# Gamma row written as 16 rows, modulation pieces spread anew, 1/rms per token block, the output projection's second half by chunk, and a moved DMA-queue wait, in a two-layer mLSTM / attention / GLA block kernel

## The chip, the cores and the metric

One NeuronCore of one Trainium2 chip runs the whole program in one launch. The metric is the device time of an execution in microseconds. Three executions of the kernel before took 2641.11, 2654.57 and 2652.0 us; their median is 2652.0 us.

## What is computed

Two layers over 256 tokens of width 2048, batch 1, all fp32. A conditioning vector gives six modulation vectors per layer; each layer is a mixer and a convolutional feed-forward, both between modulated RMS norms:

```python
cond = jax.nn.silu(c)
for layer in range(2):
    mod = (cond @ ada_w[layer] + ada_b[layer])[:, None, :]
    sh_m, sc_m, g_m, sh_f, sc_f, g_f = jnp.split(mod, 6, axis=-1)
    h = rms_norm(x, norm_w[layer, 0]) * (1.0 + sc_m) + sh_m
    y = even_mixer(h, ...) if layer == 0 else odd_mixer(h, ...)
    x = x + g_m * rms_norm(y, norm_w[layer, 1])
    h = rms_norm(x, norm_w[layer, 2]) * (1.0 + sc_f) + sh_f
    y = conv_ffn(h, ...)
    x = x + g_f * rms_norm(y, norm_w[layer, 3])
```

`even_mixer` is an mLSTM (4 heads) beside a forgetting attention (8 heads); `odd_mixer` is gated linear attention (GLA, 4 heads) with a low-rank decay gate. `conv_ffn` is a 2048 to 2x5632 projection, a causal three-tap depthwise convolution, `a * gelu(g)`, and a projection back.

## The kernel before

**Units.** All projection weights are cut into 394 units of 128x2048 fp32 (1 MB). A unit goes through a fixed chain. The SP queue loads it into one of four `raw` slots. ACT rounds it to fp32r (`hi`, L458). DVE writes the rest (`lo = raw - hi`, L851). PE multiplies `hi` by the high and low part of the activations and `lo` by the high part. There are two slots of `hi` and `lo`, so the `hi` of unit n+1 waits until PE has finished unit n-1 (`s_unit`). In every loop body step j, DVE first makes the `lo` of the *next* unit, then does whatever else belongs to step j, and last copies PE's result out of PSUM. A unit of kind "columns" (or `ff_up`) has 48 matmuls of 256 columns (L1539 to L1541); a unit of kind "tokens" (`values`, `mixed`, `ff_down`) has 24 of 512 columns (L1564 to L1566).

**Phases.** The table in `plan()` lists the phases in order; every engine walks the same table. Per layer: gates, the mixer's input projections with the mixer's own work beside them (`side`), `mixed` (the mixer's output projection, 16 units), and then three groups of `ff_up` and `ff_down` (32+16, 32+16 and 24+12 units). `ff_down` makes four chunks of 512 output columns, four units each (three in the last group). `mixed` makes its four chunks two at a time: its units alternate between chunk 0 and 1, then between 2 and 3, so that chunks complete at units 6, 7, 14 and 15 (`token_unit`).

**Modulation.** `ada_w` is cut into 384 pieces of 128x1024 (0.5 MB; 32 pieces make one of 12 sections). The first 64 are summed at the start of the program from eight slots. The other 320 are loaded into two slots (`piece`) and summed by DVE (L862, 1.2 us each) inside the phases; the fifth argument of a phase says how many in each step. In SP's queue the load of piece a+2 waits until piece a is summed (`s_mac`), and it stands behind that step's unit load. While the GLA phases run, the piece buffers hold GLA data: no pieces are summed from `PAUSE` on until `mixed` of layer 1, where SP waits for `gla_stored` before it loads two pieces anew.

**Post-norm and pre-norm.** In `mixed` and in the last `ff_down` group (the phases with `ph.sums`), ACT squares and sums each completed chunk (`square_y`, L530) and DVE multiplies it by `gamma` (`by_gamma`, L948). `gamma` (modulation gate times norm weight) lies as 128x16, channel k*128+p at partition p, and has to become a row of 2048 on every partition. ACT's queue writes it to DRAM (`gamma_row_dmas`, L539: 2048 values of 4 bytes each) and reads it back to all partitions (L542, 1 MB). The read waits on ACT for the write (`s_row_out`). ACT runs this in its own program order, between two `hi` operations: the write at step 5, the wait and the read at step 6.

After the last unit DVE reduces the squares, adds the scaled `y` to `x` in five pieces (L965), ACT squares `x` (L483, five pieces), DVE sums them over both token blocks (`x_root`, L897), ACT takes the root (L471), DVE the reciprocal and two diagonal matrices (L902). PE multiplies `x` by them: this transposes and scales at once (`x_transposes`, L1379), 24 blocks before the next phase's first unit. ACT and DVE apply the modulation (`scaled`, L494 and L913) and split the result (`high`, `low`, L504 and L920), and the first unit starts when the first pair is ready.

```python
if j == 5:
    sc.wait_ge(s_gamma, m + 1)
    with nc.allow_non_contiguous_dma("2048 values, once for each norm"):
        sc.dma_start(row_dram.rearrange("a (k p) -> p (a k)", p=P), gamma[:, :]).then_inc(s_row_out, 16)
if j == 6:
    sc.wait_ge(s_row_out, 16 * (m + 1))
```

## Time and profile before

| | |
|---|---|
| executions | 2641.11, 2654.57, 2652.0 us |
| profiled execution | 2654.36 us, span 2652.6 us |
| PE busy | 2402.4 us (91%) |
| PE weight loads busy | 2216.4 us (84%) |
| DVE busy | 1963.7 us (74%) |
| ACT busy | 1019.7 us (38%) |
| TensorE clock granted, mean | 0.965 of full |
| bytes moved | 627 MB, mean 236 GB/s |

PE is the busiest engine, and the share hides where it stops. The time is best read as a chain of phases, each of which either runs at PE's pace or at that of something that PE waits for. The profiled execution took 2.4 us more than the median.

### The profile page before, as it was taken

The numbers are of one execution on the slowest core, as the hardware profiler recorded it, in microseconds if no ns is written. First come the engines' busy times: TensorE is split into PE (matmuls) and PEld (weight loads), VectorE is DVE, ScalarE is ACT, GpSimd is POOL, SyncE is SP. The second block draws the span as 40 slices with busy tenths as digits, with TensorE's granted clock in tenths as the row PEclk, the third lists the DMA queues.
The fourth block names the chain that finished last, engine by engine and source line by source line (L and its number), as shares of the span: only waits on it lengthen the run. The fifth ranks groups of instructions, "written<-read, shape, count | busy, mean of one in ns | idle before, by whom it ended". The sixth has DMA issues, their size and how long they took to land.

```text
span 2652.6 us, 40622 instructions
## 1 busy us (share of the span) xinstructions
PE 2402.4 (91%) x16118; PEld 2216.4 (84%) x16118; DVE 1963.7 (74%) x2340; ACT 1019.7 (38%) x1001; POOL 426.2 (16%) x198
## 2 busy tenths in 40 slices
PE   0499999879999999999959999977899999999996
PEld 0488878669997999889949989966899899989994
DVE  7876886679997899789867776656899556655654
ACT  1223434444343343333435544433443334333442
POOL 0000000003430244014200000000234013411320
PEclk9799998989999999999979999989899999999997
DMA  9888774666778877887866644456577555455553
GB/s 400 337 311 293 278 273 179 197 226 236 271 284 301 288 280 268 327 291 274 280 213 244 234 157 144 143 165 249 182 275 271 191 190 186 177 190 191 185 181 94
DMA packets 122601, 627.16 MB, mean 236 GB/s; under 512 B 20960, under 2 KB 21088, under 8 KB 71280
## 3 DMA queue, kind: packets, MB, share of 16 engines
q1 hardware_dynamic: 113648, 621.22, 65.2%
q10 hardware_dynamic: 8832, 4.23, 0.6%
q8 instruction: 88, 1.44, 0.2%
q14 instruction: 33, 0.27, 0.0%
HBM read 623.27 MB, written 2.13 MB: 236 GB/s over the span
## 4 chain that ended last, share of the span: by engine, by line
PE 74%; DMA 12%; DVE 11%; ACT 2%; issue 1%; SPq 0%; DVEq 0%; ACTq 0%
PE bank L1539 16%; PE bank L1540 16%; PE bank L1541 16%; DMA piece<-ada_pieces 8%; PE bank L1564 7%; PE bank L1565 7%; PE bank L1566 7%; DVE lo L851 3%; DVE piece L862 3%; DVE region L862 1%; PE bank L1379 1%; DMA region<-ada_pieces 1%; ACT hi L458 1%; PE bank L1456 1%; DMA gamma_scratch<-gamma 1%
## 5 line engine op out<-in xcount | busy, mean ns | idle before, releaser
L458 ACT ACTIVATE hi<-raw 128x2048 fp32r<-128x2048 f32 x394 | 754.3, 1915 | 1323.6 <-PE bank L1541 794.5
L1539 PE MATMUL bank<-act,hi 128*128 128x256 f32 x3872 | 1105.2, 285 | 11.6 <-DVE lo L851 10.5
L1540 PE MATMUL bank<-act,hi 128*128 128x256 f32 x3872 | 1098.3, 284 | 0.0
L1541 PE MATMUL bank<-act,lo 128*128 128x256 f32 x3872 | 1098.2, 284 | 0.0
L851 DVE TENSOR_TENSOR lo<-raw,hi 128x2048 fp32r<-128x2048 f32 x394 | 901.7, 2289 | 237.4 <-ACT hi L458 236.8
L1539 PEld LDWEIGHTS bank<-act,hi 128*128 128x128 f32 x3872 | 746.1, 193 | 17.7 <-DVE lo L851 13.1
L1540 PEld LDWEIGHTS bank<-act,hi 128*128 128x128 f32 x3872 | 746.2, 193 | 0.3
L1541 PEld LDWEIGHTS bank<-act,lo 128*128 128x128 f32 x3872 | 745.8, 193 | 0.0
L862 DVE SCALAR_TENSOR_TENSOR piece<-piece,cond 128x1024 f32<-128x1024 f32 x320 | 452.2, 1416 | 130.5 <-DMA piece<-ada_pieces 129.9
L832 POOL TENSOR_TENSOR region<-region 128x256 f32<-128x256 f32 x88 | 204.7, 2327 | 1063.2 <-ACT region L732 1063.2
L1564 PE MATMUL bank<-hi,mid 128*128 128x512 f32 x704 | 276.9, 393 | 35.5 <-DVE lo L851 35.5
L1565 PE MATMUL bank<-lo,mid 128*128 128x512 f32 x704 | 275.4, 391 | 0.0
L1566 PE MATMUL bank<-hi,mid 128*128 128x512 f32 x704 | 275.1, 391 | 0.0
L835 POOL TENSOR_TENSOR mid<-region,mid 128x256 f32 (+1 forms) x88 | 207.6, 2359 | 276.1 <-ACT mid L736 276.1
L1564 PE MATMUL bank<-hi,act 128*128 128x512 f32 x512 | 209.0, 408 | 38.7 <-DVE lo L851 37.1
L1565 PE MATMUL bank<-lo,act 128*128 128x512 f32 x512 | 204.9, 400 | 0.0
L1566 PE MATMUL bank<-hi,act 128*128 128x512 f32 x512 | 204.2, 399 | 0.0
L1564 PEld LDWEIGHTS bank<-hi,mid 128*128 128x128 f32 x704 | 133.1, 189 | 67.2 <-DVE lo L851 39.9
L1379 PE MATMUL bank<-region,x 128*128 128x128 f32 x256 | 41.9, 335 | 145.4 <-DVE region L902 111.8
L1326 DVE TENSOR_SCALAR region<-bank,vec 128x256 f32<-128x256 f32 x176 | 95.2, 541 | 99.5 <-PE bank L1541 95.7
L1379 PEld LDWEIGHTS bank<-region,x 128*128 128x128 f32 x256 | 40.3, 249 | 146.9 <-issue 65.9
L1566 PEld LDWEIGHTS bank<-hi,mid 128*128 128x128 f32 x704 | 133.0, 189 | 28.0
(155 smaller groups left out, 1562.4 us busy)
## 6 DMA issues: line engine op xcount, KB each, us to landing
raw<-w_units SPq DMA_DIRECT2D x394, 1024.0 KB, 4.8
piece<-ada_pieces SPq DMA_DIRECT2D x320, 512.0 KB, 4.9
region<-ada_pieces SPq DMA_DIRECT2D x64, 512.0 KB, 8.7
region<-gamma_scratch ACTq DMA_DIRECT2D x4, 1024.0 KB, 7.8
x<-x_in SPq DMA_DIRECT2D x1, 2048.0 KB, 15.5
x_out<-x SPq DMA_DIRECT2D x3, 512.0 KB, 2.8
cond<-c_row SPq DMA_DIRECT2D x1, 1024.0 KB, 4.4
vec<-vectors SPq DMA_DIRECT2D x1, 534.5 KB, 11.0
```

What stands on the lines that cost most here:

```text
L458: sc.activation(hi[:, slot, :], raw[:, raw_slot, :], ACT.Copy).then_inc(s_hi, 1)
L832: gp.tensor_tensor(ff_m[:, slot, :], conv_a[:, slot, :], gelu_g[:, slot, :], ALU.mult).then_inc(s_mul, 1)
L835: gp.tensor_tensor(flat(mid[:, at_, T:2 * T]), ff_m[:, slot, :], flat(mid[:, at_, 0:T].bitcast(F32)), ALU.subtract).then_inc(s_mid, 1)
L851: ve.tensor_tensor(lo[:, slot, :], raw[:, raw_slot, :], hi[:, slot, :].bitcast(F32), ALU.subtract).then_inc(s_lo, 1)
L862: return ve.scalar_tensor_tensor(out=src, in0=src, scalar=1.0, in1=cond[:, half * PIECE:(half + 1) * PIECE], op0=ALU.mult, op1=ALU.mult, a ...
L1379: i_ = pe.matmul(bank[4 + p % 4][:, at:at + P], x[:, tb, kt * P:(kt + 1) * P], diag[:, tb, :], start=True, stop=True)
L1539: pe.matmul(dst, w_hi, act[:, kt, 0:T], start=at == 0, stop=False)
L1540: pe.matmul(dst, w_hi, act[:, kt, T:2 * T], start=False, stop=False)
L1541: i_ = pe.matmul(dst, w_lo, act[:, kt, 0:T], start=False, stop=at == DK - 1)
L1564: pe.matmul(dst, x_hi, w_hi, start=opens and q == 0, stop=False)
L1565: pe.matmul(dst, x_hi, w_lo, start=False, stop=False)
L1566: i_ = pe.matmul(dst, x_lo, w_hi, start=False, stop=closes and q == 3)
```

## The change

Seven edits, all in the order of the work; no arithmetic of the reference changes.

1. **Gamma by 16 rows.** PE transposes `gamma` into PSUM after step 1 of the phase, DVE copies the 16x128 block to SBUF (step 2 in `mixed`, step 3 in `ff_down`), ACT's queue writes it as 16 rows of 128 values at step 3, and waits and reads it back at step 5. `gate_weight` of `mixed` moves from step 4 to step 0.
2. **`by_gamma`** of chunks 0 to 2 moves from behind the copies to fixed steps (`late_gamma`).
3. **`mixed`** becomes one body of 16 steps: 8 as before, then chunk 2 in four units and chunk 3 in four.
4. **Pieces.** Another number per step in eight phases; `PAUSE` moves from 336 to 344.
5. **1/rms per token block**: `x_root` becomes `x_sum` and `x_diag`, one of each per block, between the updates of `x`; PE transposes block 0 of the first eight channel tiles before block 1 (`x_first_transposes`).
6. DVE's `lo` of the second unit of a phase with a pre-norm moves behind the pre-norm.
7. **SP's wait** for `gla_stored` moves from before `mixed` of layer 1 to its step 3, behind that step's unit load.

```diff
-        if self.kind == "mixed":
+        if self.kind == "mixed" and j < 8:
             return j % 2, tail(self)[0][j // 2], j < 2, j >= 6
         tile, g = divmod(j, self.k_units)
...
-    no, half = (0,) * 4, (2, 1) * 4
+    no, down = (0,) * 4, (1, 2, 2, 1) * 4
...
-              Phase("values", 0, 1, 8, (1,) * 8, dest=M_HEADS * M_DV),
+              Phase("values", 0, 1, 8, (2, 1) * 4, dest=M_HEADS * M_DV),
...
-              Phase("mixed", 0, 2, 8, (0, 1, 0, 0, 1, 2, 2, 2)),
-              Phase("ff_up", 0, 8, 4, (1,) * 4, 0), Phase("ff_down", 0, 2, 8, half, 0),
-              Phase("ff_up", 0, 8, 4, (1,) * 4, 1), Phase("ff_down", 0, 2, 8, half, 1),
-              Phase("ff_up", 0, 6, 4, (1,) * 4, 2), Phase("ff_down", 0, 1, 12, (1, 2, 1) * 4, 2),
+              Phase("mixed", 0, 1, 16, (0, 0, 0, 0, 1, 1, 1, 1, 1, 2, 2, 1, 1, 1, 0, 0)),
+              Phase("ff_up", 0, 8, 4, (1,) * 4, 0), Phase("ff_down", 0, 1, 16, down, 0),
+              Phase("ff_up", 0, 8, 4, (1,) * 4, 1), Phase("ff_down", 0, 1, 16, down, 1),
+              Phase("ff_up", 0, 6, 4, (1,) * 4, 2),
+              Phase("ff_down", 0, 1, 12, (1, 2, 2, 1, 2, 2, 1, 2, 2, 1, 0, 0), 2),
               Phase("gates", 1, 1, 1, (0,)),
-              Phase("columns", 1, 4, 4, (2, 1, 2, 1), dest=GQ, side="decay"),
+              Phase("columns", 1, 4, 4, (2,) * 4, dest=GQ, side="decay"),
...
-              Phase("mixed", 1, 2, 8, (0, 0, 0, 0, 1, 2, 2, 3)),
+              Phase("mixed", 1, 1, 16, (0, 0, 0, 0, 0, 1, 1, 1, 1, 1, 1, 1, 1, 0, 0, 0)),
...
+                        if ph.a0 == PAUSE and ph.kind == "mixed" and j == 3:
+
+                            sp.wait_ge(s["gla_stored"], G_HEADS)
+                            for more in range(ADA_SLOTS):
+                                load_piece(PAUSE + more, more)
...
                     sc.activation(yt[:, tb, at:at + size], x[:, tb, at:at + size], ACT.Square,
                                   accum_out=stat[:, col:col + 1]).then_inc(s_xsq, 1)
+                    if k == 1:
+                        token_root(S_RHO, 1)
+                token_root(S_RHO + 1, 1)
...
+                if j == 3:
+                    sc.wait_ge(s_rows, m + 1)
+                    sc.dma_start(row_dram.rearrange("a (k p) -> (a k) p", p=P), gamma_rows).then_inc(s_row_out, 16)
                 if j == 5:
-                    sc.wait_ge(s_gamma, m + 1)
-                    with nc.allow_non_contiguous_dma("2048 values, once for each norm"):
-                        sc.dma_start(row_dram.rearrange("a (k p) -> p (a k)", p=P), gamma[:, :]).then_inc(s_row_out, 16)
-                if j == 6:
+                    if ph.kind == "mixed":
+                        sc.wait_ge(*((s["mlstm_stored"], 2 + M_HEADS) if ph.layer == 0 else (s["gla_stored"], G_HEADS)))
                     sc.wait_ge(s_row_out, 16 * (m + 1))
...
-                for tb, at, size in X_PIECES:
+                for k, (tb, at, size) in enumerate(X_PIECES):
+                    if k == 3 and not last:
+                        x_sum(m + 1, 0)
                     x_at = x[:, tb, at:at + size]
                     ve.scalar_tensor_tensor(out=x_at, in0=yt[:, tb, at:at + size], scalar=r[:, tb:tb + 1], in1=x_at,
                                             op0=ALU.mult, op1=ALU.add).then_inc(s_x, 1)
+                if not last:
+                    x_diag(m + 1, 0)
+                    x_sum(m + 1, 1)
+                    x_diag(m + 1, 1)
...
                 if ph.norms:
+                    pre_norm(ph)
                     if ph is not PHASES[0]:
-                        x_root(2 * ph.layer + int(ph.kind == "ff_up"))
                         split_next(ph, 0, 0)
-                    pre_norm(ph)
...
+                late_gamma = (8, 9, 13) if ph.kind == "mixed" else (7, 8, 10)
...
+                        if ph.sums:
+                            if j == (2 if ph.kind == "mixed" else 3):
+                                gamma_to_rows(ph)
+                            if j in late_gamma:
+                                by_gamma(ph, late_gamma.index(j))
...
+            def x_first_transposes(q):
+                for tb in range(TB):
+                    pe.wait_ge(s_diag, TB * q + tb + 1)
+                    for kt in range(DK // 2):
+                        i_ = x_block(kt // 2, kt, tb)
+                        if tb == TB - 1 and kt % 2 == 1:
+                            i_.then_inc(s_tp, 1)
...
+                        if ph.sums and j == 1:
+                            pe.wait_ge(s_gamma, 2 * ph.layer + int(ph.kind == "ff_down") + 1)
+                            pe.transpose(bank[4][0:DK, 0:P], gamma[:, :], ident[:, :]).then_inc(s_gt, 1)
```

ACT in the last `ff_down` of layer 0, before. `hi<-raw` is the split of a unit's weights; `region,stat<-y` the squares of a chunk:

```order
L458 ACTIVATE hi<-raw 128x2048 x2
L530 ACTIVATE region,stat<-y 128x512 x2
L458 ACTIVATE hi<-raw 128x2048 x2
L539 DMA gamma_scratch<-gamma 128x16x1
L458 ACTIVATE hi<-raw 128x2048
L542 DMA region<-gamma_scratch 128x2048
L530 ACTIVATE region,stat<-y 128x512 x2
L458 ACTIVATE hi<-raw 128x2048 x3
```

And with the change:

```order
L461 ACTIVATE hi<-raw 128x2048 x2
L544 DMA gamma_scratch<-region 16x128
L536 ACTIVATE region,stat<-y 128x512 x2
L461 ACTIVATE hi<-raw 128x2048 x2
L549 DMA region<-gamma_scratch 128x2048
L461 ACTIVATE hi<-raw 128x2048
L536 ACTIVATE region,stat<-y 128x512 x2
```

The write stands two splits earlier, and two splits lie between write and read instead of one.

DVE from the last step of `mixed` of layer 0 into the pre-norm of `ff_up`, before (`piece,part` is a modulation piece, `y<-bank` the copy of a chunk):

```order
L851 TENSOR_TENSOR lo<-raw,hi 128x2048
L862 SCALAR_TENSOR_TENSOR piece,part<-piece,cond 128x1024
L1306 COPY y<-bank 128x512 x2
L948 TENSOR_TENSOR y<-y,region 128x2x512
L862 SCALAR_TENSOR_TENSOR piece,part<-piece,cond 128x1024
L948 TENSOR_TENSOR y<-y,region 128x512
L958 TENSOR_REDUCE stat<-stat 128x2
...
L965 SCALAR_TENSOR_TENSOR x<-y,stat,x 128x1024 x3
L965 SCALAR_TENSOR_TENSOR x<-y,stat,x 128x512 x2
L897 TENSOR_REDUCE stat<-stat 128x2
L884 RECIPROCAL stat<-stat 128x2
L902 TENSOR_SCALAR region<-ident,stat 128x128 x2
```

With the change:

```order
L857 TENSOR_TENSOR lo<-raw,hi 128x2048 x2
L1335 COPY y<-bank 128x512 x2
L959 TENSOR_TENSOR y<-y,region 128x512
L970 TENSOR_REDUCE stat<-stat 128x2
...
L979 SCALAR_TENSOR_TENSOR x<-y,stat,x 128x1024 x3
L902 TENSOR_REDUCE stat<-stat 128x1
L979 SCALAR_TENSOR_TENSOR x<-y,stat,x 128x512 x2
L890 RECIPROCAL stat<-stat 128x1
L908 TENSOR_SCALAR region<-ident,stat 128x128
L902 TENSOR_REDUCE stat<-stat 128x1
```

Two pieces and one full `by_gamma` left the stretch between the last unit and the updates, and the first diagonal matrix is ready before the squares of block 1 are summed.

SP around `mixed` of layer 1, before (what stands in brackets is what the issue waits for):

```order
L402 DMA raw<-w_units 128x2048 [waits lo_ready] x33
L406 DMA piece<-ada_pieces 128x1024 [waits gla_stored]
L406 DMA piece<-ada_pieces 128x1024
L402 DMA raw<-w_units 128x2048 [waits lo_ready] x5
```

With the change:

```order
L406 DMA raw<-w_units 128x2048 [waits lo_ready] x37
L410 DMA piece<-ada_pieces 128x1024 [waits gla_stored]
L410 DMA piece<-ada_pieces 128x1024
L406 DMA raw<-w_units 128x2048 [waits lo_ready] x2
```

Four more unit loads stand ahead of the wait.

## Rows read from the trace of the kernel before

**Rows 1.** The page: GB/s in 40 slices; the chain that ended last, by engine.

```profile
GB/s 400 337 311 293 278 273 179 197 226 236 271 284 301 288 280 268 327 291 274 280 213 244 234 157 144 143 165 249 182 275 271 191 190 186 177 190 191 185 181 94
...
PE 74%; DMA 12%; DVE 11%; ACT 2%; issue 1%; SPq 0%; DVEq 0%; ACTq 0%
```

**Rows 2.** Who waited for whom: us in total, times, longest.

```profile
PE bank L1379 <- DVE region L902: 111.8, 4, 65.9
...
PE bank L1564 <- DVE lo L851: 72.6, 17, 15.0
```

**Rows 3.** Stretches: length, busy time PE PEld DVE ACT POOL, clock, DMA, GB/s.

```profile
117.33:221.53 104.20, 95.76 (x771) 94.12 (x769) 76.95 (x92) 34.17 (x21) 0.00 (x0) 0.98 0.84 299
221.53:269.49 47.96, 45.77 (x197) 37.12 (x195) 33.05 (x37) 15.50 (x9) 0.00 (x0) 0.96 0.79 283
466.95:571.13 104.18, 92.21 (x384) 73.97 (x384) 68.03 (x66) 39.01 (x34) 0.00 (x0) 0.95 0.68 227
...
781.27:874.50 93.23, 89.01 (x387) 71.36 (x385) 69.69 (x75) 31.38 (x18) 3.69 (x2) 1.00 0.87 310
...
1289.33:1371.43 82.10, 67.08 (x290) 54.87 (x288) 53.39 (x56) 29.12 (x28) 3.51 (x2) 0.92 0.82 266
...
1400.64:1497.76 97.12, 97.12 (x786) 95.01 (x785) 72.84 (x84) 51.81 (x48) 0.00 (x0) 1.00 0.76 283
1728.74:1848.90 120.16, 96.41 (x394) 77.62 (x392) 65.70 (x62) 39.48 (x35) 0.00 (x0) 0.90 0.60 201
...
2558.09:2640.27 82.18, 67.84 (x290) 55.43 (x288) 32.73 (x23) 27.07 (x27) 3.15 (x2) 0.90 0.37 115
2332.79:2419.86 87.07, 87.07 (x386) 72.08 (x385) 42.04 (x25) 31.50 (x18) 3.15 (x2) 1.00 0.54 193
...
2148.48:2332.79 184.31, 184.31 (x1537) 184.31 (x1536) 119.98 (x127) 71.86 (x62) 71.32 (x30) 1.00 0.51 183
```

**Rows 4.** The chain that ended last, last ff_down of layer 0: start, us, what.

```profile
1316.84 14.45 DMA gamma_scratch<-gamma
1331.31 7.80 DMA region<-gamma_scratch
```

**Rows 5.** Timeline, mixed of layer 1: start, us, what, [idle before, releaser].

```profile
1761.83 1.91 ACT L458 ACTIVATE hi<-raw 128x2048 fp32r<-128x2048 f32 x1 [12.72 <-DMA raw<-w_units]
...
1766.12 0.80 PE L1564 MATMUL bank<-hi,act 128*128 128x512 f32 x1 [8.14 <-DVE lo L851]
...
1787.71 0.80 PE L1564 MATMUL bank<-hi,act 128*128 128x512 f32 x1 [8.93 <-DVE lo L851]
```

**Rows 6.** DMA issues: KB each, median us from issue to landing.

```profile
piece<-ada_pieces SPq DMA_DIRECT2D x320, 512.0 KB, 4.9
...
x_out<-x SPq DMA_DIRECT2D x3, 512.0 KB, 2.8
...
gamma_scratch<-gamma ACTq DMA_DIRECT2D x4, 8.0 KB, 14.2
```

**Rows 7.** Timeline from the last unit of mixed, layer 0.

```profile
573.92 1.28 DVE L1306 COPY y<-bank 128x512 f32<-128x512 f32 x2
...
579.37 5.00 DVE L965 SCALAR_TENSOR_TENSOR x<-y,stat,x 128x1024 f32<-128x1024 f32 x5
...
582.85 0.19 ACT L483 ACTIVATION_READ_ACCUMULATOR y<-x 128x1 f32 x1
...
586.75 7.85 PE L1379 MATMUL bank<-region,x 128*128 128x128 f32 x48 [15.46 <-DVE region L902]
```

**Rows 8.** Timeline, the transposes at the other two norms.

```profile
1383.96 8.57 PE L1379 MATMUL bank<-region,x 128*128 128x128 f32 x48 [12.37 <-DVE region L902]
...
1867.04 7.71 PE L1379 MATMUL bank<-region,x 128*128 128x128 f32 x48 [17.98 <-DVE region L902]
```

**Rows 9.** Timeline of DVE behind that pre-norm of layer 0.

```profile
599.00 2.48 DVE L920 TENSOR_TENSOR act<-y,act 128x512 fp32r<-128x512 f32 x4
...
604.92 2.29 DVE L851 TENSOR_TENSOR lo<-raw,hi 128x2048 fp32r<-128x2048 f32 x1 [0.43 <-ACT hi L458]
```

More of the change, by code:

```diff
@@ L435, in _ @@
                     sp.dma_start(g_w2, w2_dram).then_inc(s["loaded_a_w2"], 16)
-                if ph.a0 == PAUSE and ph.kind == "mixed":
-                    sp.wait_ge(s["gla_stored"], G_HEADS)
-                    for k in range(ADA_SLOTS):
-                        load_piece(PAUSE + k, k)
                 straight = ph.per_body > 0 and ph.a_end in (PAUSE, SECTIONS * PIECES)
@@ L939, in gate_weight, with gamma_to_rows @@
                                  ALU.mult).then_inc(s_gamma, 1)
+            def gamma_to_rows(ph):
+                m = 2 * ph.layer + int(ph.kind == "ff_down")
+                ve.wait_ge(s_gt, m + 1)
+                ve.tensor_copy(gamma_rows, bank[4][0:DK, 0:P]).then_inc(s_rows, 1)
             def by_gamma(ph, chunk, first=0, last=TB):
@@ L952, in post_norm @@
             def post_norm(ph, between):
+                last = ph is PHASES[-1]
                 m = 2 * ph.layer + int(ph.kind == "ff_down")
@@ L1233, in _ @@
                 if sec > 0:
-                    x_root(0)
+                    ve.wait_ge(s_in["ident"], 16)
+                    x_sum(0, 0)
+                    x_diag(0, 0)
+                    x_sum(0, 1)
+                    x_diag(0, 1)
                     ve.wait_ge(s_in["vec"], 16)
@@ L1309, in body @@
                             i_.then_inc(s_evac, 1)
-                            if ph.sums and ph.tiles * i + tile > 0:
-                                by_gamma(ph, ph.tiles * i + tile - 1)
                         elif ph.kind == "gates":
@@ L1369, in _, with x_block @@
         def _(pe):
+            def x_block(p, kt, tb):
+                at = (kt % 2) * T + tb * P
+                return pe.matmul(bank[4 + p % 4][:, at:at + P], x[:, tb, kt * P:(kt + 1) * P], diag[:, tb, :],
+                                 start=True, stop=True)
+            def x_first_transposes(q):
[5 more added lines that the diff above has]
+                            i_.then_inc(s_tp, 1)
             def x_transposes(q, p):
-                if p >= 4 and p % 2 == 0:
+                if p % 2 == 0:
                     pe.wait_ge(s_na, 4 * q + (p - 4) // 2 + 1)
-                if p >= 4 and p % 2 == 1:
+                else:
                     pe.wait_ge(s_nv, 4 * q + (p - 4) // 2 + 1)
@@ L1377, in x_transposes @@
                     for tb in range(TB):
-                        at = (kt % 2) * T + tb * P
-                        i_ = pe.matmul(bank[4 + p % 4][:, at:at + P], x[:, tb, kt * P:(kt + 1) * P], diag[:, tb, :],
-                                       start=True, stop=True)
+                        i_ = x_block(p, kt, tb)
                 i_.then_inc(s_tp, 1)
@@ L1514, in _ @@
                     q = 2 * ph.layer + int(ph.kind == "ff_up")
-                    pe.wait_ge(s_diag, q + 1)
-                    for p in range(6):
+                    x_first_transposes(q)
+                    for p in (4, 5):
                         x_transposes(q, p)
```

36 lines of the change are left out of this document (18 added, 18 removed).

## The prediction

> **What bounds the kernel now.** I read the page first. The chain that ended last is PE for 74% and DMA for 12% [rows 1]: PE sets the pace, and the question is where it stops. The view of waits names two stops. PE's first matmul of a token unit waits for DVE's `lo`, 72.6 us in all, and the norm transposes wait for the diagonal matrices, 111.8 us, of which 65.9 us are one harmless early wait [rows 2]. To price phases I took the pace of phases in which nothing is late: 16 token units in 87.07 us, 5.44 each, and 32 column units in 184.31 us, 5.76 each [rows 3]. What a phase takes beyond that is loss:
>
> - `mixed` of layer 0: 104.18 - 87.07 = 17.1
> - last `ff_down` of layer 0 (12 units, 65.3 at pace): 82.10 - 65.3 = 16.8
> - `mixed` of layer 1: 120.16 - 87.07 = 33.1
> - last `ff_down` of layer 1: 82.18 - 65.3 = 16.9 [rows 3].
>
> Three norm transitions follow, each with PE idle for 12.4 to 18.0 us before the transposes and 8 us of transposes [rows 7, 8].
>
> **Gamma.** The chain through the last `ff_down` of layer 0 is a write of 14.45 us and then the read-back of 7.80 [rows 4]. ACT waits in between and cannot split the next weights, so PE starves; clock is lost too (0.92 and 0.90 granted in these stretches against 1.00 [rows 3]). The new write moves the same 8 KB in 16 rows. The trace has no such DMA: the write of 4-byte values took 14.2 us, a store of 512 KB in long rows 2.8 us [rows 6]. I take 3 us, by the latter, since it differs from the old in its rows and not in its bytes; it may also be shorter or as long as before. From step 3 to the wait at step 5 are two units, 10.9 us, and the readers of the row come 2 or 3 units after that, 10.9 us or more against 7.8. So both waits end before anybody is there: the 16.8 and 16.9 go. New on this path are a transpose and a copy of 16 rows, under 0.5 us, beside other work, and in `ff_down` ACT waits at step 3 for the copy that stands behind DVE's `lo`, with its next split about 1 us late and as much slack: 0.2 each. **-33.3.**
>
> The Trainium skill, in DMA: Bandwidth & Descriptors, section Anatomy of one DMA, puts the fixed cost of a DMA at about 2.0 us, most of it the receipt of the write. By it the new write would take 2.0 us; no row here shows one, and the sum would be the same.
>
> **`mixed` of layer 0.** Of the 17.1 some 3 are the gating work of its first steps and stay. The rest, near 13.7, is the same 14 us write and the pieces that land late beside it (one, two, two and two in steps 4 to 7). It goes, but `gate_weight`, the copy and the write's issue now stand in the tight steps (0.7), and steps 9 and 10 sum two pieces each beside a `by_gamma` (1.5). **-11.5.**
>
> **`mixed` of layer 1.** Two causes. SP waits for `gla_stored` before all loads of the phase: ACT waited 12.72 us for `raw`, PE 8.14 [rows 5], with the cold clock after it 9.8 in all. Behind the new place of the wait four more units are already loading, and the last GLA head is stored in step 3 or 4, one unit before the first withheld load matters: the 9.8 go. Then the gamma write and up to three pieces a step: 8.93 once [rows 5] and 6.7 again eight units on, with their slow restarts 21.4. These go as well, since each step has one piece. About 2 remain, and 1.3 are new (the last gating part collides with a split). **-29.9.**
>
> **Transitions.** In layer 0 the last unit of `mixed` ends at 571.13 [rows 3]. DVE copies its chunk only at 573.92, since a piece is late, and begins the updates 5.45 us after that [rows 7], with `by_gamma` of chunk 2 (1.2) and a piece (1.2) in between. With neither left the copy starts at once (0.2), and the updates about 3.7 us later, as the squares of the last chunk are now waited for: 3.9 after the unit. Updates to transposes took 7.4 us (579.37 to 586.75). Now block 0 is squared 3.7 us after the updates begin (582.85 + 0.19), its sum lies between the third and the fourth update, which end with the fifth at 5.2, and reciprocal, diagonal and start add 0.7: 5.9. ACT's root delays the squares of block 1 by 0.7 us; its diagonal is due at 8.0, while the eight transposes of block 0 keep PE until 8.5 at least (7.85 / 24 = 0.33 us each on average, more at first, when PE comes from idling and has the lower clock). So PE resumes 9.8 us after the unit, where it took 15.6; 9.4 where it took 12.5 (last `ff_down`, no section to close), and 9.8 where it took 18.1 (layer 1) [rows 8]. The same 24 blocks follow, 7.8 us. Together 5.8 + 3.1 + 8.3, **-17.2**.
>
> Against that stands the `lo` that moved behind the pre-norm. It was made while DVE waited for transposes, at no cost. DVE ends the pre-norm at 601.4, and the second unit started near 602.7 (2.2 us before the `lo` of the third, at 604.92) [rows 9]. Now 2.2 us of `lo` come first, 603.6, so each such phase starts its second unit 1.0 later, three times: **+3.0.** It is bounded by 0 and 2.2 each.
>
> **The end.** One `by_gamma` less after the last copy, largely replaced by the wait for the squares: **-0.5.** At the start DVE must wait between the two diagonals for ACT's squares of block 1, about 2.9 us, but the piece loads queued ahead cover it and DVE then sums faster than they land: **+0.5**, at most 2.9.
>
> **Pieces.** What left `mixed` has gone elsewhere. With two slots, a slot's cycle is a load (4.9 us, median [rows 6], up to 7 beside a unit load) and a sum of 1.2.
>
> - `values` of layer 0, 8 to 12 pieces, 1.5 a unit. `ff_down` has this density: 93.23 - 87.07 = 6.2 lost in 16 units [rows 3]. Half of it, **+3**, bounds 0 and 6.
> - The two `ff_down` with (1, 2, 2, 1) in place of (2, 1, 2, 1): the same number, but two double steps in a row leave a slot one unit of 5.44 us for its cycle. **+1 each**, bounds -2 and +5.
> - Last `ff_down` of layer 0, 16 pieces in 10 units instead of 12. At the 3.9 us a piece (93.23 / 24) they need 62 us where PE needs 54, less what two slots already hold: **+5**, bounds 1 and 10.
> - `decay` columns of layer 1, 24 to 32 pieces, two a unit. The first column phase of layer 0 has just this and takes 104.20 us for 16 units; this one takes 97.12 [rows 3]. I take about 105: **+8**, and 1 for the later start of GLA, bounds 2 and 14.
>
> The slices of the page show 400 GB/s at the start [rows 1], so two pieces and a unit, 2.1 MB, would fit into 5.3 us; what limits is the cycle of the slots. The Trainium skill speaks otherwise, in DMA: Bandwidth & Descriptors, section Where 436 GB/s comes from: HBM gives a core some 358 GB/s. The trace disagrees, with its 400; by the page this phase would be bound at 5.86 us a unit and cost 1.6 instead of 8.
>
> **Sum.** -33.3 - 11.5 - 29.9 - 17.2 - 0.5 = -92.4, and 3 + 0.5 + 3 + 2 + 5 + 9 = +22.5: **-69.9**. Against the profiled execution's 2654.4 that is 2584.5; the median lies 2.4 below it, so I say **2582**.
>
> **Rivals.** *The pieces cost twice as much.* DVE, SP and the queue are in order, and a late piece delays the next `lo`: for it speaks that losses in `ff_down` come from waits for pieces, against it that PE has a unit of slack here and there. The 19 us of pieces become 38: 2601. Chance 0.17.
>
> *The write stays slow* (12 us or more, since it is a write to DRAM and not its rows that cost). ACT then waits some 4 us at step 5 in four phases, 3.5 each on PE: 2596. The store of 2.8 us speaks against it. Chance 0.08.
>
> *The stalls return cheaper than I think*, with PE's clock up all through `mixed` and denser pieces hidden: the piece terms vanish, 2563. Chance 0.13.
>
> *Slower than before:* the slot cycle becomes the bound. Some 108 of the pieces lie in phases with 1.5 or more a unit (12 + 24 + 24 + 16 + 32); two slots make each microsecond of cycle worth half a microsecond a piece, 54 us. It would take 83 us on top, 1.5 us on every cycle, to pass 2652 by 0.5%: 2665 or more. Nothing shows such a cycle, 8 us on average. Chance 0.01.
>
> *The change doesn't do what it says:* the row still comes late, since ACT stands at step 3 behind PE's transpose and DVE's copy for a unit or more. Gamma's term would halve: 2600, within the range; 0.03.
>
> **Numbers.** My own case has 0.58, with its bounds 2566 to 2598. The range of 0.8 takes in the cheap rival in part and most of the dear ones: 2562 to 2604. A measurement of this kernel tells about 0.5% (13 us) from no change: faster 0.97, same 0.02, slower 0.01.
>
> **What would show it.** Right: the write `gamma_scratch` under 4 us; no idle of PE above 3 us inside any `mixed` or last `ff_down`; the two `mixed` at 93 and 90 us, the last `ff_down` of layer 0 and 1 at 70 and 66; PE's idle before the transposes 9.5 us three times; first units of these phases near 9 us; `decay` at 105. Wrong: a new wait of ACT at step 3 or 5, PE idle behind pieces over 40 us in sum, or transposes that wait for the second diagonal.

## The result and the profile after

Four executions of the changed kernel took 2576.94 to 2580.99 us, median 2579.84, beside 2649.7 for the kernel before on the same chip. The ratio is 0.9738, 95% interval 0.971 to 0.9766: faster, by about 70 us. The prediction was 2582 (2562 to 2604). The profiled execution took 2580.99 us, span 2579.2, against 2654.36 and 2652.6 before: 73.4 us less.

The page of the changed kernel, GB/s in 40 slices and the chain by engine, against [rows 1]:

```profile
GB/s 397 339 316 305 286 286 197 214 209 266 271 272 323 294 275 271 307 300 277 287 266 226 297 147 147 132 178 279 187 274 272 196 182 185 186 181 195 180 184 141
...
PE 73%; DMA 11%; DVE 11%; ACT 2%; issue 1%; DVEq 0%; SPq 0%; ACTq 0%
```

The shares of the chain have hardly moved, and the page alone would not show where 73 us went. The stretches do. The view of windows, columns as in [rows 3]; in this order: `values` and `mixed` of layer 0, `ff_down` groups 0 and 1 of layer 0, the last `ff_down` of layer 0, the decay columns, `mixed` of layer 1, the last `ff_down` of layer 1:

```profile
221.07:270.76 49.69, 46.24 (x194) 37.12 (x195) 36.53 (x42) 14.72 (x8) 0.00 (x0) 0.97 0.84 308
465.88:556.42 90.54, 88.16 (x385) 71.75 (x385) 68.95 (x64) 38.76 (x34) 0.00 (x0) 1.00 0.69 256
762.08:853.67 91.59, 88.11 (x386) 71.58 (x384) 69.50 (x75) 32.55 (x19) 3.69 (x2) 1.00 0.87 316
1038.08:1130.54 92.46, 88.33 (x387) 71.59 (x385) 69.79 (x75) 33.13 (x19) 3.37 (x2) 1.00 0.86 312
1269.10:1344.47 75.37, 69.20 (x291) 55.12 (x289) 55.48 (x60) 28.88 (x28) 3.69 (x2) 0.95 0.82 299
1369.91:1475.28 105.37, 99.83 (x784) 96.73 (x785) 78.75 (x97) 51.00 (x48) 0.00 (x0) 0.98 0.89 302
1711.33:1800.63 89.30, 89.30 (x395) 73.41 (x393) 62.69 (x54) 39.28 (x35) 0.00 (x0) 1.00 0.68 247
2502.22:2567.70 65.48, 65.48 (x291) 53.89 (x289) 34.23 (x25) 27.09 (x27) 3.15 (x2) 1.00 0.39 144
```

Read each length against its row in [rows 3]. `mixed` of layer 0 fell from 104.18 to 90.54 and that of layer 1 from 120.16 to 89.30; in the latter PE is now busy for the whole stretch, at the full granted clock, where it had 0.90. The last `ff_down` of layer 1 fell from 82.18 to 65.48, its pace. That of layer 0 fell by 6.7 only and keeps a clock of 0.95: something still stops PE there. The decay columns grew from 97.12 to 105.37.

DMA issues, KB each and median us to landing, against [rows 6]:

```profile
region<-gamma_scratch ACTq DMA_DIRECT2D x4, 1024.0 KB, 7.1
...
gamma_scratch<-region ACTq DMA_DIRECT2D x4, 8.0 KB, 3.3
```

The write of the same 8 KB takes 3.3 us in the median where it took 14.2; the four of this execution took 1.9 to 5.1 us.

The norm transition of layer 0, timeline, against [rows 7] (the last unit of `mixed` ends at 556.42):

```profile
556.62 1.29 DVE L1335 COPY y<-bank 128x512 f32<-128x512 f32 x2 [1.14 <-PE bank L1604]
...
560.08 3.68 DVE L979 SCALAR_TENSOR_TENSOR x<-y,stat,x 128x1024 f32<-128x1024 f32 x3
...
563.85 1.41 DVE L979 SCALAR_TENSOR_TENSOR x<-y,stat,x 128x512 f32<-128x512 f32 x2
...
565.71 8.36 PE L1399 MATMUL bank<-region,x 128*128 128x128 f32 x48 [9.13 <-DVE region L908]
```

The copy comes 0.2 us after the unit (it was 2.8), the updates 3.7 (8.2) and PE 9.3 (15.6). From the updates to PE it is 5.6 us, where it was 7.4. The waiting line shrank as well, from the 111.8 of [rows 2]:

```profile
PE bank L1399 <- DVE region L908: 93.1, 4, 66.1
```

Two places came out worse than predicted. The first is unit 6 of the last `ff_down` of layer 0. DVE's timeline, and then the pieces (`piece`) of the stretch 1296 to 1310:

```profile
1308.42 1.23 DVE L868 SCALAR_TENSOR_TENSOR piece<-piece,cond 128x1024 f32<-128x1024 f32 x1 [5.12 <-DMA piece<-ada_pieces]
...
1311.91 2.29 DVE L857 TENSOR_TENSOR lo<-raw,hi 128x2048 fp32r<-128x2048 f32 x1
```

```profile
DMA to landing us min/median/max: 3.8/8.5/9.7
```

DVE stands 5.12 us before a piece, and the next `lo` behind it is late; PE then waits 5.2 us. The piece was issued at 1298.69, 1.4 us after ACT's read-back of the row (1 MB, 1297.32) and 1.1 us after the load of a unit, and took 9.7 us where 4.9 is the median. The second place is the start of GLA:

```profile
1477.55 1.23 DVE L868 SCALAR_TENSOR_TENSOR piece<-piece,cond 128x1024 f32<-128x1024 f32 x1 [2.52 <-DMA piece<-ada_pieces]
...
1479.63 1.22 DVE L868 SCALAR_TENSOR_TENSOR piece<-piece,cond 128x1024 f32<-128x1024 f32 x1
...
1480.89 0.63 ACT L587 ACTIVATE piece<-region 128x512 f32<-128x512 f32 x1 [8.92 <-DVE piece L868]
```

GLA uses the piece buffers, so ACT waits until the last piece is summed, 8.92 us, and makes the next `hi` only after that, at 1482.47. The first GLA unit took 13.7 us; before the change it took 8.6.

### The profile page after: what moved, and what is told of

Same layout as the page of the kernel before. It is cut to its first block, busy times and chain, and to the rows that moved or that the text cites. A ratio compares the mean times of both kernels' runs of the same rounds, so it can differ in the third digit from the quotient of the medians.

```text
span 2579.2 us, 40654 instructions
## 1 busy us (share of the span) xinstructions
PE 2389.8 (93%) x16122; PEld 2206.3 (86%) x16122; DVE 1963.8 (76%) x2352; ACT 1019.5 (40%) x1005; POOL 425.4 (16%) x198
## 2 busy tenths in 40 slices
DMA packets 114473, 627.16 MB, mean 243 GB/s; under 512 B 12768, under 2 KB 12960, under 8 KB 63152
## 4 chain that ended last, share of the span: by engine, by line
PE 73%; DMA 11%; DVE 11%; ACT 2%; issue 1%; DVEq 0%; SPq 0%; ACTq 0%
PE bank L1577 15%; PE bank L1578 15%; PE bank L1579 15%; DMA piece<-ada_pieces 9%; PE bank L1602 8%; PE bank L1603 8%; PE bank L1604 8%; DVE lo L857 3%; DVE piece L868 3%; ACT hi L461 1%; DVE region L868 1%; DMA region<-ada_pieces 1%; PE bank L1494 1%; PE bank L1399 1%; DVE x L979 1%
## 5 line engine op out<-in xcount | busy, mean ns | idle before, releaser
L1602 PE MATMUL bank<-hi,mid 128*128 128x512 f32 x704 | 276.7, 393 | 10.8 <-DVE lo L857 10.7
L1602 PE MATMUL bank<-hi,act 128*128 128x512 f32 x512 | 204.0, 398 | 7.3 <-DVE lo L857 5.7
L1604 PE MATMUL bank<-hi,act 128*128 128x512 f32 x512 | 200.2, 391 | 0.0
L1603 PEld LDWEIGHTS bank<-lo,mid 128*128 128x128 f32 x704 | 132.8, 189 | 26.9
```

The costliest lines, as they stand in the source:

```text
L1602: pe.matmul(dst, x_hi, w_hi, start=opens and q == 0, stop=False)
L1603: pe.matmul(dst, x_hi, w_lo, start=False, stop=False)
L1604: i_ = pe.matmul(dst, x_lo, w_hi, start=False, stop=closes and q == 3)
```

## The experiments

Nine kernels ran, and the changed kernel once more. In the comparisons the kernel before had medians of 2643 to 2655 us, so a difference between two groups is given twice, by the medians and by the ratios (of 2650 us, against 0.9738 and 0.9753, the two of the changed kernel), and phases are compared by their stretches. The interval of a ratio is 5 to 10 us to either side.

**The changed kernel once more** (a_again), five executions.

> The changed kernel once more, unedited, beside the next run on one chip. If what phases with many pieces differ by from run to run (up to 3 us each) is scatter of the DMA, its phases without pieces repeat to 0.1 us and those with pieces do not, and its ratio to the kernel before lies in 0.971 to 0.979. If the 9 to 12 us that the run with the early 4-byte write lost are that write's, all its phases repeat to 1 us.

Median 2580.86, ratio 0.9753 (0.9728 to 0.9777). The first reading holds. Phases without pieces repeat to 0.03 us, but for the first unit of GLA, which waits for the pieces ahead of it. Those with pieces do not: `ff_down` group 1 took 87.68 against 92.46, the fox values 61.43 against 58.29, the last `ff_down` of layer 0 73.17 against 75.37. Any difference under some 5 us in one such phase is no evidence.

**Gamma alone, on the kernel before.**

```diff
+                if j == 3:
+                    sc.wait_ge(s_rows, m + 1)
+                    sc.dma_start(row_dram.rearrange("a (k p) -> (a k) p", p=P), gamma_rows).then_inc(s_row_out, 16)
                 if j == 5:
-                    sc.wait_ge(s_gamma, m + 1)
-                    with nc.allow_non_contiguous_dma("2048 values, once for each norm"):
-                        sc.dma_start(row_dram.rearrange("a (k p) -> p (a k)", p=P), gamma[:, :]).then_inc(s_row_out, 16)
-                if j == 6:
...
-                            if j == 4:
+                            if j == 0:
                                 gate_weight(ph.layer, 0)
...
+                        if ph.kind == "ff_down" and ph.sums and j in (7, 8, 10):
+                            by_gamma(ph, (7, 8, 10).index(j))
```

> The kernel before with gamma's new path alone: transpose after step 1, copy, 16 rows written at step 3, read back at step 5, and in ff_down by_gamma at steps 7, 8, 10. Pieces, phase bodies, norms and SP's wait stay as before. My theory (the slow write and its wait on ACT cost most): the last ff_down of layer 1 falls from 82.2 to 66 us, that of layer 0 from 82.1 to 68 to 72, mixed of layer 0 from 104.2 to about 95, mixed of layer 1 from 120.2 to about 110 (SP's wait and its bursts of pieces stay): 50 us less in all, about 2600. Rival (bursts of pieces are what starves PE in both mixed): only the two ff_down fall, 28 us less, about 2622.

Median 2602.14, ratio 0.9828 (0.9797 to 0.986): 41 us less than the kernel before by the medians, 46 by the ratio, where 50 were expected. Its stretches `mixed` 0, last `ff_down` 0, `mixed` 1, last `ff_down` 1:

```profile
469.00:566.73 97.73, 90.54 (x385) 72.62 (x385) 68.28 (x67) 38.86 (x34) 0.00 (x0) 0.98 0.66 242
1281.35:1350.98 69.63, 67.58 (x291) 54.91 (x289) 54.07 (x58) 28.89 (x28) 3.69 (x2) 0.98 0.81 312
...
1708.99:1821.64 112.65, 96.49 (x395) 77.90 (x393) 64.59 (x61) 39.48 (x35) 0.00 (x0) 0.91 0.58 214
2531.72:2597.23 65.51, 65.51 (x291) 53.89 (x289) 34.23 (x25) 27.08 (x27) 3.15 (x2) 1.00 0.38 144
```

Against [rows 3] that is 6.5 + 12.5 + 7.5 + 16.7 = 43 us, in the order of the phases. The rival, 28 us from the two `ff_down` alone, falls: both `mixed` gain too. They gain 14 where I expected 19. In the last `ff_down` of layer 0 this gain leaves 4.3 us over the pace of 65.3, with the old numbers of pieces.

**The row form alone**, written at step 5 and read at step 6 as before.

```diff
                 if j == 5:
-                    sc.wait_ge(s_gamma, m + 1)
-                    with nc.allow_non_contiguous_dma("2048 values, once for each norm"):
-                        sc.dma_start(row_dram.rearrange("a (k p) -> p (a k)", p=P), gamma[:, :]).then_inc(s_row_out, 16)
+                    sc.wait_ge(s_rows, m + 1)
+                    sc.dma_start(row_dram.rearrange("a (k p) -> (a k) p", p=P), gamma_rows).then_inc(s_row_out, 16)
```

> The kernel before with the row form alone: same steps as before for write (5) and read (6), gamma transposed after step 4, copied at step 5. If the form sets the stall, the write falls from 14.2 us to 5 or less and each of the four phases gives back about 9 us: 35 less, about 2615. If only the early start matters (the write was hidden there or the bytes cost, not their form), less than 10 us.

Median 2616.16, ratio 0.9899 (0.9864 to 0.9934): 27 us less than the kernel before.

```profile
462.58:558.44 95.86, 88.66 (x385) 71.60 (x385) 68.71 (x67) 38.95 (x34) 0.00 (x0) 1.00 0.68 247
1272.62:1349.39 76.77, 68.26 (x291) 55.66 (x289) 53.87 (x58) 29.12 (x28) 3.51 (x2) 0.93 0.77 285
...
1706.04:1815.37 109.33, 92.67 (x395) 75.66 (x393) 65.66 (x63) 39.37 (x35) 0.00 (x0) 0.92 0.58 221
2524.14:2598.18 74.04, 68.61 (x291) 55.90 (x289) 32.91 (x24) 27.19 (x27) 3.15 (x2) 0.95 0.33 128
```

8.3 + 5.3 + 10.8 + 8.1 = 32.6 us in these stretches, close to the 35 expected, though the medians differ by 27 only. The form is worth three quarters of gamma's 43 us without any earlier start. In the last `ff_down` of layer 1 half of the stall is left (8.1 of 16.7 gone), as the row is still late there: DVE waits 6.1 us for it.

**The old form, early, in the changed kernel.**

```diff
                 if j == 3:
-                    sc.wait_ge(s_rows, m + 1)
-                    sc.dma_start(row_dram.rearrange("a (k p) -> (a k) p", p=P), gamma_rows).then_inc(s_row_out, 16)
+                    sc.wait_ge(s_gamma, m + 1)
+                    with nc.allow_non_contiguous_dma("2048 values, once for each norm"):
+                        sc.dma_start(row_dram.rearrange("a (k p) -> p (a k)", p=P), gamma[:, :]).then_inc(s_row_out, 16)
...
-                            if j == (2 if ph.kind == "mixed" else 3):
-                                gamma_to_rows(ph)
```

> The changed kernel with gamma written as before, 2048 values of 4 bytes straight from the 128x16 tile, but at step 3. My theory: the write takes 14 us again, ACT waits 3 us or somewhat more at step 5 in four phases, and the time rises by 8 to 14 us over the changed kernel's 2580. If the form is everything: 30 or more. If the early start is everything: no difference, within 3 us.

Median 2591.07, ratio 0.9804 (0.9784 to 0.9824): 11 us by the medians, 14 to 17 by the ratios, so at or above the end of the 8 to 14 that I had expected, and not for the reason given. The four stretches are 92.87, 77.78, 89.23 and 65.30, only 4.5 us more than the changed kernel's. `mixed` of layer 1 and the last `ff_down` of layer 1 lose nothing: there ACT's wait at step 5 is covered. The stall that there is, in the last `ff_down` of layer 0, shows something else. DVE's timeline:

```profile
1306.14 1.23 DVE L869 SCALAR_TENSOR_TENSOR piece<-piece,cond 128x1024 f32<-128x1024 f32 x1 [8.35 <-DMA piece<-ada_pieces]
```

DVE waits 8.35 us for a piece, while the write of 4-byte values is in flight (issued 1292.50, 13.8 us). The four pieces issued from then to 1311 landed after 9.9 us in the median and 12.8 at most. The rest lies in phases with pieces and without gamma, so it may be scatter.

**The write by itself** (e9_write_alone). So I put three writes that nobody needs into the changed kernel.

```diff
+                        probe = probes.get((ph.layer, ph.group)) if ph.kind == "ff_down" else None
+                        if probe and j == 3:
+                            if probe == 2:
+                                sc.dma_start(row_dram.rearrange("a (k p) -> (a k) p", p=P),
+                                             ident[0:DK, 0:P]).then_inc(s_probe, 16)
+                            else:
+                                with nc.allow_non_contiguous_dma("2048 values of 4 bytes"):
+                                    sc.dma_start(row_dram.rearrange("a (k p) -> p (a k)", p=P),
+                                                 ident[:, 0:DK]).then_inc(s_probe, 16)
+                        if probe and j == 8:
+                            sc.wait_ge(s_probe, 16 * probe)
```

> The changed kernel with three writes that nobody needs and nobody waits for before five steps later, each at step 3 of a ff_down without a gamma: 2048 values of 4 bytes in layer 0, group 0 (pieces beside it) and in layer 1, group 0 (no pieces), 16 rows of 512 bytes in layer 0, group 1 (pieces beside it). Theory A (a write of 4-byte values holds up the other loads while it is in flight, beside the wait of ACT): loads issued in its 13 us land after 10 us or more where the median is 4.9; the first phase takes 97 to 101 us where it took 91.3 to 91.6, from one stall at its units 4 to 6; that of layer 1 stays at 87.07, since four raw slots cover it; the one with the row write stays in 87.7 to 92.5. Sum: 5 to 9 us over 2580. Theory B (the 4-byte write costs only through ACT's wait): loads keep 5 to 7 us, all three phases stay within their scatter, 2580.

Median 2595.26, ratio 0.978 (0.9743 to 0.9817): 15 us over the changed kernel by the medians, 7 to 11 by the ratios. The three phases (4-byte with pieces, rows with pieces, 4-byte without pieces):

```profile
767.27:871.77 104.50, 91.31 (x386) 73.34 (x384) 69.50 (x75) 31.39 (x18) 3.69 (x2) 0.93 0.87 275
1056.94:1147.11 90.17, 88.22 (x386) 71.69 (x385) 69.78 (x75) 31.52 (x18) 3.37 (x2) 1.00 0.88 320
2022.83:2109.90 87.07, 87.07 (x387) 72.08 (x386) 42.65 (x29) 31.38 (x18) 3.28 (x2) 1.00 0.63 193
```

DVE in the first of them:

```profile
800.81 1.22 DVE L881 SCALAR_TENSOR_TENSOR piece<-piece,cond 128x1024 f32<-128x1024 f32 x1 [11.28 <-DMA piece<-ada_pieces]
```

Theory A holds, and its price was set too low. The first phase takes 104.5 us, 13 more than the 91.3 to 91.6 it took twice (92.2 to 93.6 in the five other traces with these numbers of pieces), and no engine ever waited for that write: DVE waits 11.28 us for a piece, and PE 10.2 behind it, then restarts at the low clock (0.93 over the stretch). Landing times of the loads issued while each write was in flight, 4-byte with pieces, rows, 4-byte without pieces: units (`raw`) 11.7 to 14.9, 4.8 to 6.9, 12.2 to 13.8 us; pieces 14.7, 4.9 to 5.3, none. Only the 4-byte form holds up others. Without pieces PE does not notice, since four `raw` slots cover 13 us.

The view of windows, six us until the first 4-byte write takes effect and eight in its midst (the last two columns are the busy share of the DMA engines and GB/s):

```profile
780.00:786.00 6.00, 6.00 (x28) 4.99 (x27) 3.43 (x2) 2.28 (x2) 0.00 (x0) 1.00 0.99 369
789.00:797.00 8.00, 5.96 (x25) 4.43 (x24) 0.53 (x1) 3.50 (x2) 0.00 (x0) 1.00 0.93 47
```

The DMA engines are nearly as busy as before, 0.93 against 0.99, and move an eighth of the bytes. The kernel before shows the same in its last `ff_down` of layer 0: 41 GB/s from 1326 to 1331, with a share of 0.85. So a busy DMA share is no sign that loads advance.

The Trainium skill, DMA: Bandwidth & Descriptors, section Queues, rings and completion order, says that a DMA engine serves its queues in turn, a packet at a time. The runs agree with it in direction: loads of another queue stretch to about the length of the 4-byte write. The same page of the Trainium skill, in Why small descriptors are slow, names two overheads, about 3 cycles a packet and 32 bytes of descriptor data for each operation. By the second, 2048 values would carry 64 KB more, an estimate of 0.2 us at the 369 GB/s above; the write took 14.4 us, and the measurement decides.

**SP's wait back before `mixed` of layer 1.**

```diff
-                        if ph.a0 == PAUSE and ph.kind == "mixed" and j == 3:
-
-                            sp.wait_ge(s["gla_stored"], G_HEADS)
-                            for more in range(ADA_SLOTS):
-                                load_piece(PAUSE + more, more)
...
+                if ph.a0 == PAUSE and ph.kind == "mixed":
+
+                    sp.wait_ge(s["gla_stored"], G_HEADS)
+                    for k in range(ADA_SLOTS):
+                        load_piece(PAUSE + k, k)
```

> The changed kernel with SP's wait for the last GLA head back before mixed of layer 1. My theory: ACT waits some 12 us for raw in the first steps, PE 8, mixed of layer 1 takes about 9.8 us more (99 where it takes 89.3): 2590. Rival (with the pieces spread, the loads catch up beside the wait): under 3 us.

Median 2597.98, ratio 0.981 (0.978 to 0.984): 17 us over the changed kernel by the medians, 15 to 19 by the ratios, where 10 were expected. The stretch takes 101.37 us against 89.30, 12.1 more:

```profile
1748.56 1.91 ACT L462 ACTIVATE hi<-raw 128x2048 fp32r<-128x2048 f32 x1 [14.27 <-DMA raw<-w_units]
...
1752.85 0.79 PE L1603 MATMUL bank<-hi,act 128*128 128x512 f32 x1 [9.69 <-DVE lo L858]
```

The mechanism is the predicted one, a little dearer than the 9.8. The few us beyond the 12.1 lie in phases with pieces and are not explained. The rival falls.

**One 1/rms for both blocks.**

```diff
-                    if k == 1:
-                        token_root(S_RHO, 1)
-                token_root(S_RHO + 1, 1)
...
-                    x_diag(m + 1, 0)
-                    x_sum(m + 1, 1)
-                    x_diag(m + 1, 1)
+                    x_root(m + 1)
```

> The changed kernel with one 1/rms for both token blocks again; the order of the transposes stays. My theory: from the first update to PE's first transpose 7.4 us where the changed kernel has 5.6, three times, so 5.4 more: 2585. Rival (the first unit waits for the pre-norm on DVE and ACT, and the transposes only queue ahead of it): nothing, within 1 us a norm.

Median 2585.75, ratio 0.9769 (0.9746 to 0.9793): 5 us more by the medians, 4 to 8 by the ratios. The timeline at the norm of layer 0:

```profile
556.87 5.00 DVE L984 SCALAR_TENSOR_TENSOR x<-y,stat,x 128x1024 f32<-128x1024 f32 x5
...
564.24 2.07 PE L1399 MATMUL bank<-region,x 128*128 128x128 f32 x8 [10.88 <-DVE region L904]
```

7.37 us from updates to PE, 5.63 in the changed kernel: 1.7 us, as predicted for a norm, and the first units start 1.5 to 2.8 us later (from the start of the last unit to that of the next phase 24.98, 24.58 and 24.01 us, against 23.31, 21.74 and 22.54; against the second run of the changed kernel it is 0.9 to 2.2). The rival falls.

**`lo` ahead of the pre-norm again.**

```diff
-                    pre_norm(ph)
                     if ph is not PHASES[0]:
                         split_next(ph, 0, 0)
+                    pre_norm(ph)
```

> The changed kernel with DVE's lo of the second unit again ahead of the pre-norm. My theory: DVE is idle there until the first transposes, so the lo costs nothing, and each of the three phases starts its second unit 1.0 us sooner: 3.1 less, 2577. Rival (lo is still running when the first transposes are done, and the first unit starts later by what it overlaps): 0 to 2 us more.

Median 2575.62, ratio 0.973 (0.9708 to 0.9752): 4 to 5 us less by the medians, 2 to 6 by the ratios. Each of the three first units takes 8.11 us where it took 9.15, 3.1 in all, as in the kernel before. The transitions ahead of them are no longer than in the other traces, so the rival's later first unit doesn't show. The ratio alone could not tell that from nothing; the trace can. This part of the change is a loss.

**The old numbers of pieces in the changed kernel.**

```diff
-              Phase("columns", 1, 4, 4, (2,) * 4, dest=GQ, side="decay"),
+              Phase("columns", 1, 4, 4, (2, 1, 2, 1), dest=GQ, side="decay"),
...
-              Phase("mixed", 1, 1, 16, (0, 0, 0, 0, 0, 1, 1, 1, 1, 1, 1, 1, 1, 0, 0, 0)),
+              Phase("mixed", 1, 1, 16, (0, 0, 0, 0, 1, 2, 2, 3) * 2),
```

(and so for the other phases of the table)

> The changed kernel with the numbers of pieces per step as before in all phases. My theory: what left the mixed phases costs elsewhere about what it saved. Back come some 5 us in mixed of layer 0 and 8 in mixed of layer 1; away go 8 in the decay columns, 5 at the start of GLA, 2 in values and 2 to 3 in the last ff_down of layer 0: the sum is within 6 us of the changed kernel, 2574 to 2586. Rival (bursts in mixed are a cause of their own, as in the 8.93 us stalls): 20 us more, 2600.

Median 2586.99, ratio 0.9784 (0.9757 to 0.981): 6 to 7 us more by the medians, 8 to 12 by the ratios, outside my interval of 6; the rival's 2600 lies above the interval of the ratio. Stretches: the last `ff_down` of layer 0, decay columns, `mixed` of layer 1:

```profile
1269.46:1342.07 72.61, 68.84 (x291) 55.66 (x289) 54.47 (x59) 28.89 (x28) 3.70 (x2) 0.95 0.78 301
...
1368.42:1465.64 97.22, 97.22 (x784) 95.11 (x785) 72.67 (x84) 51.03 (x48) 0.00 (x0) 1.00 0.80 293
1696.45:1799.90 103.45, 93.11 (x395) 75.23 (x393) 68.16 (x64) 39.50 (x35) 0.00 (x0) 0.95 0.64 235
```

The decay columns give back 8.2 and the first GLA unit 5.2 (8.46 us). `mixed` of layer 1 costs 14.2 more, not 8, and the transition behind it 6.8 more (29.32 from the start of the last unit to the next phase, where it was 22.54); its last step sums three pieces again. `mixed` of layer 0 costs 2.9, not 5. So bursts of three do stall PE by themselves, also with the fast write; but the phases to which the pieces went pay most of it back.

The last `ff_down` of layer 0 has only its old numbers here and still takes 7.3 us over its pace. DVE's timeline at the same place as in the changed kernel:

```profile
1307.32 1.23 DVE L868 SCALAR_TENSOR_TENSOR piece<-piece,cond 128x1024 f32<-128x1024 f32 x1 [5.06 <-DMA piece<-ada_pieces]
```

It waits 5.06 us for a piece, as against 5.12 with the new numbers. Units 6 and 7 lose 6.4 us here and 4.0 with gamma alone; in the six traces with the new numbers and the fast write they lose 3.3 to 8.8. So most of this stall doesn't come from the denser pieces.

**Other numbers of pieces** (e8_pieces_anew), with `lo` ahead of the pre-norm.

```diff
-              Phase("columns", 0, 2, 4, (1,) * 4, dest=MO, side="mlstm"),
+              Phase("columns", 0, 2, 4, (1, 1, 2, 2), dest=MO, side="mlstm"),
...
-              Phase("ff_down", 0, 1, 12, (1, 2, 2, 1, 2, 2, 1, 2, 2, 1, 0, 0), 2),
+              Phase("ff_down", 0, 1, 12, (2, 2, 2, 1, 1, 1, 1, 2, 2, 1, 1, 0), 2),
...
-              Phase("columns", 1, 4, 4, (2,) * 4, dest=GQ, side="decay"),
+              Phase("columns", 1, 4, 4, (2, 1, 2, 1), dest=GQ, side="decay"),
...
-              Phase("mixed", 1, 1, 16, (0, 0, 0, 0, 0, 1, 1, 1, 1, 1, 1, 1, 1, 0, 0, 0)),
+              Phase("mixed", 1, 1, 16, (0, 0, 0, 0, 0, 1, 1, 1, 1, 1, 2, 2, 1, 1, 1, 0)),
```

> The changed kernel with lo ahead of the pre-norm and other numbers of pieces: the last ff_down of layer 0 has one a step around the read-back of the row (steps 3 to 6) and two before and after it; the decay columns have 24 as before the change; the mlstm columns take 4 more and mixed of layer 1 takes 12. My theory: the 7.8 us that units 6 and 7 of that ff_down lose go, as their two pieces no longer share the queues with the 1 MB read-back (75.4 becomes 68); decay columns 97 where they took 105.4 and the first GLA unit 9 where it took 13.7; mlstm columns and mixed of layer 1 cost 2 and 2 more; with 3 for the lo the sum is 20 less than the changed kernel's, 2560. Rival (the queue is short of slots all through that ff_down and not only beside the read-back; pieces put elsewhere cost what they cost here): 5 less, 2575.

Median 2559.26, five executions, ratio 0.9682 (0.9659 to 0.9705); the changed kernel on the same chip had 2580.86 and 0.9753. This is the fastest of the study, 21.6 us under the changed kernel by the medians, 19 by the ratios, where 20 were expected. Stretches: mlstm columns, the last `ff_down` of layer 0, decay columns, `mixed` of layer 1:

```profile
389.73:462.08 72.35, 69.62 (x480) 62.36 (x478) 59.19 (x107) 34.06 (x49) 3.00 (x4) 0.95 0.63 224
...
1262.98:1333.86 70.88, 67.78 (x291) 54.71 (x289) 56.23 (x60) 29.12 (x28) 3.37 (x2) 0.98 0.87 318
1359.36:1456.48 97.12, 97.12 (x786) 95.01 (x785) 72.74 (x84) 51.79 (x48) 0.00 (x0) 1.00 0.76 283
1687.50:1777.18 89.68, 89.65 (x395) 73.34 (x393) 67.18 (x62) 39.28 (x35) 0.00 (x0) 1.00 0.73 269
```

The decay columns are back at 97.12 and the first GLA unit at 8.68 us. The four more pieces in the mlstm columns (DMA share 0.63 where the changed kernel has 0.54 there) and the four in `mixed` of layer 1 cost nothing that shows: 72.35 against 74.56, and 89.68 against 89.30. In the last `ff_down` unit 6 loses nothing any more, although pieces issued beside the read-back still took 6.6 to 8.9 us: with one a step they are not yet waited for. In steps 3 to 6 the old numbers have one double step, those of the changed kernel two, and these none. Units 9 and 10, behind two double steps, lose 4.3 instead. So the phase gains 2.3 to 4.5, not the 7 I expected (68), and no more than its scatter; units 6 and 7, at 5.44 us each, are the better sign. There the rival is partly right, two slots are short wherever two double steps meet.

## Why the prediction was right, point by point

| Term | predicted | measured |
|---|---|---|
| last `ff_down` of layer 0 (-16.6 for gamma, +5 for pieces) | -11.6 | -6.7 |
| last `ff_down` of layer 1 | -16.7 | -16.7 |
| `mixed` of layer 0 | -11.5 | -13.6 |
| `mixed` of layer 1 | -29.9 | -30.9 |
| three transitions | -17.2 | -19.1 |
| `lo` behind the pre-norm | +3.0 | +3.1 |
| `values` of layer 0 | +3 | +1.7 |
| two `ff_down` with (1, 2, 2, 1) | +2 | -0.1 |
| decay columns | +8 | +8.3 |
| start of GLA | +1 | +5.1 |
| start and end of the program | 0 | -0.1 |
| sum | -69.9 | -69.0 |

The two profiled executions differ by 73.4; the other 4.4 lie in column, attention and `ff_up` phases, where the second run of the same kernel moved as much.

- **Gamma.** The write takes 3.3 us where I said 3 (1.9 to 5.1, on both sides of the 2.0 that it quotes), and both waits of ACT are gone. In layer 1 all of the 16.7 went. In layer 0 it is the term that was mis-sized, 12.5 with gamma alone where 16.6 were put down (see below), so the two `ff_down` gave 29.2 and not 33.3. The mechanism was half told: I priced the old write by ACT's wait alone. It also held up all loads of SP's queue, which the writes of the experiment that nobody waits for show (13 us with pieces beside them).
- **The rival "the write stays slow"** put 3.5 us on each of four phases through ACT's wait. With the old form at step 3 three of the four lose 2.3 us or nothing, and the fourth stalls for a piece. Its price of 14 came near the 11 to 17 measured, by another mechanism.
- **`mixed` of layer 1.** SP's wait was worth 12.1, not 9.8, so gamma and the pieces brought 18.8 where 20.1 were predicted (21.4 less the 1.3 that were new).
- **Transitions.** PE resumed 9.3 us after the unit, against 9.8 predicted. The saving by block, 7.4 to 5.9, was 7.4 to 5.6. The `lo` cost its 1.04 each.
- **Last `ff_down` of layer 0**, mis-sized. I expected PE at its pace but for "+5" of the denser pieces; it is 10 us over in one execution and 8 in the other. The step that was wrong is that "the 16.8 and 16.9 go": of the 16.8 they don't. With gamma alone and the old pieces 4.3 us stay, and the changed kernel with the old pieces keeps 7.3: a piece issued beside the row's read-back lands late, and PE then waits. My sign "no idle of PE above 3 us" failed here too (5.2). The two traces with the old numbers and the fast write have 69.6 and 72.6 us, the six with the new ones 73.1 to 76.9; by the means the denser pieces add near 4, about the +5.
- **Start of GLA**, mis-sized: "1 for the later start" measured 5.1. I had priced the pieces by PE's pace in the phase before, and not followed who waits for the last of them: ACT, which makes the next `hi` only after its copies into the piece buffers.
- **Decay columns.** They cost 8.3, as the slots' cycle gave, and not the 1.6 of a bound by 358 GB/s.
- **The rival "pieces cost twice as much"** falls. The terms of the pieces measured 1.7, -0.1, near 4, 8.3 and 5.1, in all 19, which is what I had put down for them; the start of GLA was dearer than said and the others cheaper.
- **Luck.** The sum held in part by errors that cancel: +4.9 in the last `ff_down` of layer 0 and +4.1 at the start of GLA, against -2.1, -1.9, -1.0, -1.3 and -2.1 elsewhere.

## What to carry to other kernels

A small write whose elements scatter as 4-byte packets is not a matter of its own latency: find out which loads are in flight beside it, and give it long rows (here one transpose and one copy). A high busy share of the DMA engines doesn't tell that bytes move; look at the GB/s of the same stretch. Price a table of prefetches by its bursts and by who waits for the last one, not by the mean per step; a phase whose pace is set by other work (here the mlstm columns) took more at no cost that showed. And follow a sum term by term in the trace, as a right total may hide two wrong terms.

## What the runs showed that I had not expected

- 2048 values of 4 bytes to DRAM, 8 KB, take 11.5 to 15.0 us (ten writes in three traces), and in e9 1 MB loads of another queue issued beside them take 11.7 to 14.9 us instead of 4.9, a load of 512 KB 14.7. 16 rows of 512 bytes take 1.3 to 5.7 us, and loads beside one of them stayed at 4.8 to 6.9. Which property of the 4-byte form costs, the number of packets or their size, no run separates. In the kernel before, the packets under 512 bytes were 20960, now 12768: 8192 fewer, which is 2048 for each of the four writes.
- Pieces issued beside a 1 MB read-back from DRAM to all partitions and the load of a unit took up to 8.9 and 9.7 us, where 4.9 is the median. No run takes the read-back away, so its share in this is not shown.
- The same kernel's phases with many pieces differ by up to 5 us between two executions, while phases without them repeat to 0.03 us. Some of this is not a spread but two values: the fox values take 58.3 or 61.5 us in all twelve traces.
